# Hybrid decoder step on one core: VectorE's softmax first in its beat, weight splits of the beat three ahead inside it, level exponents ahead of the last level's take, decay sums spread

## What is computed

```python
h = rms_norm(x, norm_g)
a_q, a_k, a_v, a_z, b_u, b_z, c_q, c_k, c_v, c_lr, c_z, gates = split(h @ w_in)
# A: 16 query heads, 4 key heads of 64, q/k norm, rotary, window 128, a learned sink in the softmax
o_a = sink_attention(rope(norm(a_q)), rope(norm(a_k)), a_v, sinks)
# B: causal means over 2/4/8/16 tokens minus the token, a 256x256 map for each of 4 groups
o_b = multiscale_pool(b_u) * pool_scale
# C: gated linear attention, 4 heads, dk 128, dv 256
log_a = log_sigmoid(c_lr @ w_gate_lr + b_gate) / 16
o_c = rms_norm(gla(c_q, c_k, c_v, log_a), gla_norm_g)
br = stack(o_a * silu(a_z), o_b * silu(b_z), o_c * silu(c_z)) @ w_branch
y = x + (sum over branches of sigmoid(gates) * br) @ w_out
```

## Time and profile before

| | |
|---|---|
| median of 3 runs | 2437.93 us (2436.49 to 2440.85) |
| the profiled execution, its own time | 2442.46 us |
| its span, first to last instruction | 2440.7 us |
| PE busy | 2382.1 us, 98% |
| DVE busy | 1374.5 us, 56% |
| ACT busy | 1012.4 us, 41% |
| POOL busy | 71.9 us, 3% |
| mean granted clock of TensorE | 0.983 of full speed |
| DMA | 360.68 MB, mean 148 GB/s |

### The profile page before, as it was taken

How to read it: one execution, slowest core, us unless ns; L and a number is a source line. 1 busy time by engine, 2 the same in 40 slices (tenths; PEclk the granted TensorE clock), 3 DMA queues, 4 the chain that set the end, 5 groups by cost and what they waited for, 6 DMA issues and landing times.

```text
span 2440.7 us, 38676 instructions
## 1 busy us (share of the span) xinstructions
PE 2382.1 (98%) x16192; PEld 2334.3 (96%) x16192; DVE 1374.5 (56%) x2324; ACT 1012.4 (41%) x1813; POOL 71.9 (3%) x110
## 2 busy tenths in 40 slices
PE   6999999899999999999999999998999999999998
PEld 6999999799999999999999999998999999999998
DVE  5666656665545455546656675666555455554443
ACT  5335345654333333333342442456443333333332
POOL 0010000000000000000000100000000000000000
PEclk9999999999999999999999998999999999999999
DMA  6333554223444444445553434532244444444453
GB/s 256 113 112 131 187 194 136 90 93 117 152 147 152 151 147 151 152 147 189 195 203 104 147 131 171 189 121 94 80 138 148 153 149 148 153 149 148 153 201 121
DMA packets 97134, 360.68 MB, mean 148 GB/s; under 512 B 11376, under 2 KB 11376, under 8 KB 96128
## 3 DMA queue, kind: packets, MB, share of 16 engines
q1 hardware_dynamic: 85824, 312.51, 38.6%
q0 software_dynamic: 9840, 43.02, 4.8%
q10 hardware_dynamic: 1296, 2.67, 0.3%
HBM read 341.59 MB, written 20.50 MB: 148 GB/s over the span
## 4 chain that ended last, share of the span: by engine, by line
PE 87%; DVE 6%; ACT 3%; issue 2%; DMA 1%; ACTq 0%; POOL 0%; DVEq 0%; POOLq 0%
PE main L1382 79%; PE side L1382 8%; DVE w_lo L380 2%; ACT w_hi L961 1%; ACT probs L1118 1%; PE side L1386 1%; DMA x_first<-in_x_pairs 1%; ACT tc L1158 1%; DVE small L698 0%; DVE probs L693 0%; DVE ta L395 0%; DVE cb L544 0%; DVE probs L721 0%; DVE xg_lo L415 0%; DVE lev_e L558 0%
## 5 line engine op out<-in xcount | busy, mean ns | idle before, releaser
L1382 PE MATMUL main<-xg_hi,w_hi 128*128 128x320 f32 x3488 | 1105.4, 317 | 22.8 <-DVE w_lo L380 20.5
L380 DVE TENSOR_TENSOR w_lo<-raw,w_hi 128x512 fp32r<-128x512 f32 x1192 | 794.3, 700 | 538.7 <-ACT w_hi L961 527.5
L1382 PE MATMUL main<-xg_lo,w_hi 128*128 128x320 f32 x3488 | 1088.1, 312 | 0.0
L1382 PE MATMUL main<-xg_hi,w_lo 128*128 128x320 f32 x3488 | 1087.6, 312 | 0.0
L961 ACT ACTIVATE w_hi<-raw 128x512 fp32r<-128x512 f32 x1192 | 715.8, 627 | 711.3 <-PE main L1382 698.5
L1382 PEld LDWEIGHTS main<-xg_hi,w_hi 128*128 128x128 f32 x3488 | 665.3, 191 | 33.9 <-DVE sq_sum L423 16.7
L1382 PEld LDWEIGHTS main<-xg_lo,w_hi 128*128 128x128 f32 x3488 | 665.3, 191 | 2.0
L1382 PEld LDWEIGHTS main<-xg_hi,w_lo 128*128 128x128 f32 x3488 | 664.2, 190 | 0.0
L1382 PE MATMUL main<-branch_hi,w_hi 128*128 128x320 f32 x768 | 237.3, 309 | 0.0
L1382 PE MATMUL main<-branch_lo,w_hi 128*128 128x320 f32 x768 | 237.3, 309 | 0.0
L1382 PE MATMUL main<-branch_hi,w_lo 128*128 128x320 f32 x768 | 237.3, 309 | 0.0
(11 more groups left out here) (218 smaller groups left out, 1459.2 us busy)
## 6 DMA issues: line engine op xcount, KB each, us to landing
raw<-in_w_stream SPq DMA_DIRECT2D x596, 512.0 KB, 3.3
state<-in_state POOLq DMA_DIRECT2D x16, 512.0 KB, 6.2
out_state_s<-state POOLq DMA_DIRECT2D x16, 512.0 KB, 3.0
x_first<-in_x_pairs ACTq DMA_DIRECT2D x8, 320.0 KB, 16.3
w_pool<-in_w_pool POOLq DMA_DIRECT2D x2, 1024.0 KB, 10.7
cache_k<-in_cache_k POOLq DMA_DIRECT2D x2, 1024.0 KB, 5.8
cache_v<-in_cache_v POOLq DMA_DIRECT2D x2, 1024.0 KB, 8.9
out_k_window<-in_cache_k_tok POOLq DMA_DIRECT2D x2, 960.0 KB, 9.9
```

The lines of the kernel that those rows point to most:

```text
L380: dve.tensor_tensor(w_lo[Q % RAWS][:, half], raw[Q % RAWS][:, half], w_hi[Q % HIS][:, half].bitcast(F32), ALU.subtract).then_inc(lo_ready, 1)
L1382: return pe.matmul(out, lhsT, rhs, start=start, stop=stop)
```

## The change

It does five things to the order, and adds or removes no arithmetic, no matmul and no DMA.

1. `log_decay_sum` keeps only the two elementwise instructions at beat 12; the four scans move to beat 13 (`decay_scan`), the two clears to beat 15 (`clear_scores`).
2. `level_prep(k)` stands ahead of `level_take(k - 1)` in the same beat. It gets a wait for DVE's own earlier instructions (`v.settle()`), which the take had given it.
3. `prompt_softmax` and `sample_softmax` move out of `vector_part` and stand behind `split_lo(Q + 2)`, ahead of all else at that beat (`vector_softmax`).
4. In beats that have scores (`scored_at`), the split of block Q + 3 follows: on ACT right behind that of Q + 2 and ahead of `scalar_part`, on DVE behind the softmax. The next beat then has no split.
5. Splits are counted (`split_lo_to`, `split_hi_to`), so that a block is split once; in the gate, branch and output beats this renames the call and changes no order.

```diff
@@ -135,6 +135,12 @@
 TAKE.update({g: first_beat(g) + 4 for g in range(G_CZ, G_AZ + 1)})
 TAKE.update({27: 115, 28: 118})
+
+def scored_at(beat):
+
+    return any(n in ("scores", "sample_scores") for n, _, _ in STEPS.get(beat, ()))
+
+
 TAKEN_AT = {b: g for g, b in TAKE.items()}
 
@@ -372,6 +378,14 @@
             free = [0]
 
+            lo_next = [0]
+
+            def split_lo_to(Q):
+
+                while lo_next[0] <= min(Q, BEATS * DEPTH - 1):
+                    split_lo(lo_next[0])
+                    lo_next[0] += 1
+
             def split_lo(Q):
 
@@ -540,9 +554,13 @@
                 v(dve.tensor_scalar(lev_q[:, :, :], lev_q[:, :, :], 0.0, 1.0 / 16.0, ALU.min, ALU.mult))
                 v.settle()
                 stt(lev_q[:, :, :], lev_e[:, :, :], -1.0 / 16.0, lev_q[:, :, :], ALU.mult, ALU.add)
+
+            def decay_scan(l):
                 for h in range(GH):
                     v(dve.tensor_tensor_scan(cb[:, h, :], keep, lev_q[:, h, :], 0.0, ALU.mult, ALU.add))
                 v.settle()
+
+            def clear_scores(l):
                 v(dve.memset(att_p[:, :, :], 0.0))
                 v(dve.memset(att_s[:, :], 0.0))
                 v.settle()
@@ -555,6 +573,7 @@
                 if k > 1:
                     dve.wait_ge(level_k, 7 * l + k - 1)
+                    v.settle()
                 v(dve.tensor_tensor(e4, b4, b4[:, :, :, B - 1:B].to_broadcast([P, GH, n, 2 * B]), ALU.subtract))
                 v.mark("level_gap", l, k)
@@ -762,6 +781,14 @@
                     elif name == "sample_scores":
                         sample_probs(l, k)
+
+            def vector_softmax(l, beat):
+
+                for name, k, _ in STEPS.get(beat, ()):
+                    if name == "scores":
+                        prompt_softmax(l, k)
+                    elif name == "sample_scores":
+                        sample_softmax(l, k)
 
             def vector_part(l, beat):
@@ -787,6 +814,10 @@
                 if beat == 12:
                     log_decay_sum(l)
+                if beat == 13:
+                    decay_scan(l)
+                if beat == 15:
+                    clear_scores(l)
                 if beat == 14:
 
@@ -803,8 +834,10 @@
                     if beat == TAKE[G_U + gi] + 1:
                         pool_diff(l, gi)
-                for k in range(8):
-                    if k and beat == 18 + 2 * k:
+                for k in range(1, 8):
+                    if beat == 17 + 2 * k:
+                        level_prep(l, k)
+                    if beat == 18 + 2 * k:
                         level_scale(l, k)
                 for name, k, _ in STEPS.get(beat, ()):
@@ -826,19 +859,12 @@
                     elif name in ("k_norm", "q_norm"):
                         rope_pair(l, name, k)
-                    elif name == "scores":
-                        prompt_softmax(l, k)
-                    elif name == "sample_scores":
-                        sample_softmax(l, k)
                 if TAKEN_AT.get(beat, 0) >= G_CZ:
 
...
                     gate_product(l, GATED[-1])
                     gate_low(l, GATED[-1])
-                for k in range(1, 8):
-                    if beat == 17 + 2 * k:
-                        level_prep(l, k)
                 if beat == 34:
                     carry_prep(l)
@@ -911,12 +936,15 @@
                         first_x(0)
                         first_x(1)
-                        split_lo(0)
+                        split_lo_to(0)
                         first_x(2)
                         first_x(3)
-                        split_lo(1)
+                        split_lo_to(1)
                     vector_probs(l, beat)
-                    split_lo(Q + 2)
+                    split_lo_to(Q + 2)
+                    vector_softmax(l, beat)
+                    if scored_at(beat):
+                        split_lo_to(Q + 3)
                     vector_part(l, beat)
                 v.mark("branches", l, 0)
@@ -950,6 +978,14 @@
                                                                  act_func_set_id=LN_EXP_TABLE))
                     table[0] = LN_EXP_TABLE
+
+            hi_next = [0]
+
+            def split_hi_to(Q):
+
+                while hi_next[0] <= min(Q, BEATS * DEPTH - 1):
+                    split_hi(hi_next[0])
+                    hi_next[0] += 1
 
             def split_hi(Q):
@@ -1221,19 +1257,20 @@
                         first_x(0)
                         first_x(1)
-                        split_hi(0)
+                        split_hi_to(0)
                         first_x(2)
                         first_x(3)
-                        split_hi(1)
-                    split_hi(Q + 2)
+                        split_hi_to(1)
+                    split_hi_to(Q + 2)
+                    if scored_at(beat):
+                        split_hi_to(Q + 3)
                     scalar_part(l, beat)
                 for j in range(PAIRS):
...
                 Q0 = BEATS * l + IN_BEATS + MIX_BEATS
                 for b in range(OUT_BEATS):
-                    if Q0 + b + 2 < BEATS * DEPTH:
-                        split_hi(Q0 + b + 2)
+                    split_hi_to(Q0 + b + 2)
```

More of the change, by code:

```diff
@@ L862, in mix_pair @@
                     for part in range(6):
-                        split_lo(Q0 + 6 * n + part + 2)
+                        split_lo_to(Q0 + 6 * n + part + 2)
                         if part == 3:
@@ L887, in out_pair @@
                 for part in range(4):
-                    if Q0 + part + 2 < BEATS * DEPTH:
-                        split_lo(Q0 + part + 2)
+                    split_lo_to(Q0 + part + 2)
                 y = (ta, tb)[j % 2]
@@ L1212, in mix_pair @@
                     for part in range(6):
-                        split_hi(Q0 + 6 * n + part + 2)
+                        split_hi_to(Q0 + 6 * n + part + 2)
                         if part == 3:
```

## The result

| us | before | changed |
|---|---|---|
| median | 2438.35 (2436.49 to 2440.85, 4 runs) | 2399.35 (2398.64 to 2402.11, 4 runs) |
| profiled execution, its own time | 2442.46 | 2398.64 |
| its span | 2440.7 | 2396.9 |
| mean granted clock | 0.983 | 0.993 |

The ratio is 0.9842 with an interval of 0.9824 to 0.9859: 39 us gained in these medians, where 30.5 were forecast from a median of 2437.9. The kernel is 1.6% faster, as forecast in kind, and by more. 2399.35 lies 8 us under the forecast time of 2407.5 and 1.65 us under the lower end of the range, 2401.

The account below looks back on a forecast made before the run. PE, busy 98% of the span, bounds the kernel; only its stalls and low clock can be won. 3.9 + 5.5 + 6.8 + 12.6 + 1.7 = 30.5 us off 2437.9 gives 2407.5 us, range 2401 to 2420.

Parts of the forecast that it names:

- Decay, 3.9: Beat 15 of each layer: scans and clears moved behind its split end PE's 1.97 us stall; 3.9 us for both layers.
- Level stalls, 5.5: Level steps: exponents ahead of the copies out of PSUM end all 4 PE waits on scaled queries; 5.5 us.
- The clock behind level 1, 6.8: Behind the level step of beat 21: without the stall the clock stays up, 3.4 us a layer, 6.8 us; other end 0.
- The rival (the clock falls all the same): Level steps: small matmuls, not the stall, lower the clock; 22 us gained, 2415.9 us; chance 0.20.
- The rule weighed against it: Skill's rule: only idle gaps longer than any seen lower the clock; the low stretches would stay, sum 8.5 us smaller.
- all six stretches begin within 0.7 us of a stall: Low-clock stretches at beat 21 and at transposes, both layers: their closeness to stalls was the reason to go against the rule.
- Softmax and splits, 12.6: Scored pairs' transposes: softmax first and splits made ahead shorten the ACT and DVE chain by 6.3 us a layer, 12.6 us.
- the clock behind the fifth pair, 1.7: Behind the fifth pair's transpose: low clock costs 1.65 us a layer; one of two layers counted gained, 1.7, ends 0 and 3.3.
- The rival that the turns are held by something else: Softmax turns: PE's scores or table loads hold them; only decay and levels gain, 16.2 us, 2421.7 us; chance 0.12.
- the slower one: Scored beats: ACT's early split blocks the exponentials, costing 31 us against 16.2 gained, 2452.7 us; chance 0.03.
- The failed step: Range: low clock in steps without stalls may shift by one stretch, 3.4 us, either way, giving 2401 and 2420.
- the sum's 0 for these steps: Samples' steps, where the clock falls without stalls: the sum counted no gain there.

Follow-up runs that it names:

- each half of the part: Changed kernel without the splits of the block three ahead, 2407.87 us; changed kernel with the softmax back at its old place, 2408.16 us.
- filled: Kernel before with 18 and 24 useless matmuls in the stalls ahead of the fourth and fifth pair's transposes: ratio 1.0011.

## Why the prediction was right, and where it was wrong

**Decay, 3.9.** 4.5 in the profile, 3.9 measured alone. No new wait on a split came: the split for beat 16 had the room that was counted out.

**Level stalls, 5.5.** Right. The waits on `lev_q` are 0, and the room of 3.3 us ahead of PE is what the working gave (104.8 against 108.14).

**The clock behind level 1, 6.8.** Right as a mechanism, too large as a size. The rival (the clock falls all the same) is refuted: the level part alone takes the fall away, and none of 22 passes with the new order has it, against 14 of 14 with the old. One reading behind the term was too neat: that all six stretches begin within 0.7 us of a stall holds for this one execution (the first begins 0.8 us behind its stall), while in others the fall behind level 1 comes up to 2.4 us later or only at level 2. The rule weighed against it (the Trainium skill, TensorE: Matmul & The Clock Gate, "Why this matters for your kernels"), by which these gaps are too short, is not what the traces show: the clock fell behind idle times of 1.25, 1.70 and 1.95 us. But 6.8 us of low clock in each layer is the worse of two cases that come equally often; the term is some 5.1 on average.

**Softmax and splits, 12.6, and the clock behind the fifth pair, 1.7.** 15.4 together in the profile, against 14.3. The pieces stand as worked out: 1.17 us left at the fourth pair (1 forecast), 1.16 at the fifth (1.7), 1.33 in the first three of layer 0 together (1). Waits on probabilities came to 7.7 ("some 7"). The clock behind the fifth pair was taken as half gained; it is gained in both layers, 3.3, which leaves 12.1 of the 15.4 for the 12.6. One new wait, 0.44 us a layer for ACT's copy behind its two splits, was not forecast: the working named exponentials that the early split might block, not the copy for the value product. The rival that the turns are held by something else is refuted (each half of the part is worth 4.7 us or more), the slower one too: ACT still stands idle between its early split and the exponentials at all of the prompt's pairs, 0.45 to 2.80 us. The fifth pair is the closest (ACT's timeline after, the first pair's and the fifth's exponentials):

```profile
395.48 0.51 ACT L1154 ACTIVATE probs<-probs,small 128x256 f32<-128x256 f32 x1 [2.45 <-DVE small L726]
...
458.94 0.51 ACT L1154 ACTIVATE probs<-probs,small 128x256 f32<-128x256 f32 x1 [0.46 <-DVE small L726]
```

**The failed step** is the last one, in the chances: "where the clock falls in the steps without stalls may shift by one stretch either way with the new timing (3.4 us ...)", and with it the sum's 0 for these steps. In the pair of profiled executions they gave 11.1 us, by the means over all passes further down 4.3. (The range's lower end was also rounded down: both clocks gained, 2405.8, less 3.4 is 2402.4, not 2401.) Two things were missed. First, the base: the profiled execution of before, 2442.46, is slower than every one of its 77 timed executions over all experiments (2430.43 to 2442.12, median 2436.0), and it has 20.5 us of low clock in beats 53 to 69 of both layers where the mean of such kernels is 11.5. Durations were taken from one execution as if low clock in it were a property of the kernel. The forecast did take off 4.5 us for the slower execution, but only from the time, and not from the terms read from it. Second, beats 103 to 121 gained 1.3 us a layer that the sum did not have.

**The account.** The changed kernel's 8 executions have a median of 2401.3 (0.3 us inside the range), those of before 2436.0: a gain of 34.7 us against 30.5. Means over all profiled passes with the old and the new order of a stretch give, for both layers:

| beats | old, new passes | gain | forecast |
|---|---|---|---|
| 12 to 18, decay | 16, 22 | 3.8 | 3.9 |
| 19 to 35, levels | 14, 22 | 11.3 | 12.3 |
| 82 to 102, softmax | 14, 10 | 15.2 | 14.3 |
| 103 to 121, samples | 14, 8 | 2.5 | 0 |
| 53 to 69, samples | 16, 22 | 1.8, not shown apart from chance | 0 |

That is 34.6, of which the edited stretches are 30.3, where 30.5 were forecast. That this agrees so well is in part luck: the clock term behind level 1 was some 1.7 too large, and the one behind the fifth pair 1.6 too small. Of the 8 us by which the forecast time missed, 4.2 are gain, 1.9 are the starting median (2437.9 from 3 runs, against 2436.0), and 1.9 that the first 4 executions of the changed kernel lie under the median of 8. The range had room for one stretch; it needed the scatter of both kernels, of which the three times of before, 4.4 us apart, were a sign.

**The better kernel.** With the splits moved at beat 94 the median of 9 executions (2393.6 to 2401.13) is 2397.85, 3.4 us under the 2401.3 of the changed kernel and 38.1 under 2436.0. Its gain in beats 82 to 102 is 2.6 us a layer in the profile. The ratios do not tell the two kernels apart: 0.9841 and 0.9844, against 0.9861 of the changed kernel beside the first, but 0.9842 of it in the first result. So it is shown that the stalls end and that these beats are shorter; that the whole is faster by some 3 us is likely and not shown. What is left of waits beside the start are the 0.6 us stalls of the second and third pair.

## What to carry to other kernels

On an engine that is never idle for long, look for the short stalls at the joints between stages, and price each with the clock behind it: here a stall of 1.7 us cost another 2.5 us or so on average, at that step or the next. Put what nobody waits for behind what PE waits for, at each of the two engines of a chain that alternates, and then look for the next user that stands behind the moved piece. Before low-clock time of one profile goes into a sum, see whether it stands at the same beats in both layers and in another execution. Here the falls behind the stalls of 2.2 and 2.8 us did, and those in the steps of beats 53 to 69 did not.

## What the runs showed of the hardware that was not expected

- Executions of one and the same kernel spread over 12 us (2430.43 to 2442.12). This goes with the granted clock: in 73 of them it was 0.983 to 0.988, and those at 0.983 took 2441.4 us on average, those at 0.988 took 2431.5. Beside the stretch at the very end, the profile of before has 75.1 us of low clock, that of after 23.9.
- The length of a stall does not decide alone whether the clock falls behind it. All profiled passes counted, with a fall that begins between the last 0.3 us of the stall and 2.6 us behind it:

| stall of PE | length, us | passes | clock fell behind it |
|---|---|---|---|
| beat 15, ahead of full-size matmuls | 1.95 to 1.97 | 11 | 1 |
| level 1 | 1.69 to 1.70 | 14 | 11 |
| level 2 | 1.22 to 1.37 | 5 | 5 |
| level 3 | 1.04 to 1.15 | 11 | 0 |
| transposes of the second and third pair | 1.47 to 1.54 | 29 | 0 |
| transposes of the fourth pair | 2.49 to 2.86 | 14 | 14 |
| the same, softmax at its old place or filled | 1.81 to 1.97 | 4 | 3 |
| transposes of the fifth pair | 2.13 to 2.17 | 14 | 14 |

What else decides is open; it was not tried apart.

- With eleven useless matmuls in a stall the kernel was 2 us faster; the fall of the clock stood behind the next stall, of 1.25 us, in both layers.
- In beats 103 to 121 the low clock comes to 13.7 us in every pass of the kernels with the old softmax, though PE never waits there for more than 0.12 us; the beats at which it falls differ by one or two between passes. In beats 53 to 69 both the amount and the beats come and go.
